# Head sums of a second attention layer in their own step, decay sums by scans on VectorE, and values' transposes later in a unit

## What is computed

```python
# layer 1, gated linear attention: decays of a head's 128 keys, summed along time
log_a = jax.nn.log_sigmoid(p_a @ gla_gate_up[l] + gla_gate_bias[l]) / GLA_TAU
bcum = jnp.cumsum(at, axis=2)                 # differences of these sums decay keys and queries
# layer 2: queries and keys are normed per head of 64 before attention
qa, ka, va, qb, kb, vb = _split(h @ w_in, EVEN_SPLITS)
qa = _rmsnorm(qa.reshape(B, S, A_KV_HEADS, A_GROUP, HEAD_DIM), qn_a)
ka = _rmsnorm(ka.reshape(B, S, A_KV_HEADS, HEAD_DIM), kn_a)
qb = _rmsnorm(qb.reshape(B, S, B_HEADS, HEAD_DIM), qn_b)
kb = _rmsnorm(kb.reshape(B, S, B_HEADS, HEAD_DIM), kn_b)
```

## Time and profile before

| what | value |
|---|---|
| median of 3 runs | 2407.9 us (2406.82 to 2408.54) |
| the profiled execution | 2407.05 us, span 2405.3 us |
| PE busy | 2368.6 us, 98% of the span |
| DVE, ACT, POOL busy | 1315.1, 928.3, 159.4 us (55%, 39%, 7%) |
| PE, layer 2's stretch 1064 to 1210 | busy 130.4 of 146 us |
| weights read | 201.94 MB, 16 DMA engines busy about 28% |

### The profile page before, as it was taken

The page is one execution under the profiler, slowest core; times in us unless marked ns, Lnnn a source line. Parts: engine busy times, 40 slices in busy tenths (PEclk is TensorE's granted clock), DMA queues, the critical chain, the costliest instruction groups (busy, mean ns, idle before and its releaser), DMA issues.

```text
span 2405.3 us, 32851 instructions
## 1 busy us (share of the span) xinstructions
PE 2368.6 (98%) x13012; PEld 1922.5 (80%) x13012; DVE 1315.1 (55%) x1928; ACT 928.3 (39%) x1459; POOL 159.4 (7%) x197
## 2 busy tenths in 40 slices
PE   8999999999999999998999999999999999999999
PEld 6787777787888888875678888888888887888887
DVE  7666555878653443567764334356655556534433
ACT  5444553447242332446554223233322223422321
POOL 5111100000000000052220000000000000100000
PEclk9999999999999999999999999999999999999999
DMA  4222222222323333321023233232222212323322
GB/s 158 71 71 71 67 67 88 78 64 82 103 88 97 105 89 97 102 88 44 25 83 112 88 97 105 87 92 83 80 70 88 79 53 79 113 89 105 96 87 79
DMA packets 60639, 205.80 MB, mean 86 GB/s; under 512 B 7249, under 2 KB 7249, under 8 KB 60386
## 3 DMA queue, kind: packets, MB, share of 16 engines
q1 hardware_dynamic: 59760, 202.93, 27.6%
q10 hardware_dynamic: 754, 1.14, 0.2%
HBM read 201.94 MB, written 2.10 MB: 85 GB/s over the span
## 4 chain that ended last, share of the span: by engine, by line
PE 52%; DVE 2%; ACT 1%; issue 0%; POOL 0%; POOLq 0%; DVEq 0%; ACTq 0%
PE psum L1651 46%; PE psum L1712 1%; PE psum L1808 1%; PE psum L1719 1%; PE psum L1761 1%; ACT arena L769 1%; PE psum L1729 0%; PE psum L1725 0%; DVE arena L1287 0%; DVE cols L1293 0%; PE psum L1678 0%; PE psum L1779 0%; PE psum L1697 0%; PE psum L1734 0%; POOL stage L637 0%
## 5 line engine op out<-in xcount | busy, mean ns | idle before, releaser
L1651 PE MATMUL psum<-hhi,whi 128*128 128x512 f32 x1640 | 650.0, 396 | 11.8 <-DVE wlo L1014 9.2
L1651 PE MATMUL psum<-hlo,whi 128*128 128x512 f32 x1640 | 643.2, 392 | 0.0
L1651 PE MATMUL psum<-hhi,wlo 128*128 128x512 f32 x1640 | 642.0, 391 | 0.0
L1651 PE MATMUL psum<-uhi,whi 128*128 128x512 f32 x1392 | 548.2, 394 | 0.6 <-DVE arena L1094 0.6
L1651 PE MATMUL psum<-ulo,whi 128*128 128x512 f32 x1392 | 545.6, 392 | 0.0
L1651 PE MATMUL psum<-uhi,wlo 128*128 128x512 f32 x1392 | 545.4, 392 | 0.0
L1014 DVE TENSOR_TENSOR wlo<-raw,whi 128x1024 fp32r<-128x1024 f32 (+1 forms) x399 | 465.6, 1167 | 61.7 <-ACT whi L980 31.9
L1651 PEld LDWEIGHTS psum<-hhi,whi 128*128 128x128 f32 x1640 | 308.5, 188 | 78.6 <-issue 12.3
L1651 PEld LDWEIGHTS psum<-hhi,wlo 128*128 128x128 f32 x1640 | 308.5, 188 | 64.9 <-issue 0.4
L1651 PEld LDWEIGHTS psum<-hlo,whi 128*128 128x128 f32 x1640 | 308.8, 188 | 62.5 <-issue 1.2
L980 ACT CAST whi<-raw 128x1024 fp32r<-128x1024 f32 x190 | 199.9, 1052 | 351.7 <-PE psum L1651 351.7
(11 more groups left out here) (231 smaller groups left out, 1754.0 us busy)
## 6 DMA issues: line engine op xcount, KB each, us to landing
raw<-in_packed_dram SPq DMA_DIRECT2D x359, 512.0 KB, 3.6
raw<-in_packed_dram SPq DMA_DIRECT2D x40, 256.0 KB, 2.6
x<-in_xt_dram SPq DMA_DIRECT2D x8, 256.0 KB, 5.3
out_dram<-x SPq DMA_DIRECT2D x8, 256.0 KB, 2.0
arena<-in_near_bias_dram ACTq DMA_DIRECT2D x1, 1024.0 KB, 5.7
vec<-in_vec_dram ACTq DMA_DIRECT2D x1, 44.0 KB, 4.1
arena<-in_gla_gate_up_dram ACTq DMA_DIRECT2D x1, 32.0 KB
arena<-in_gla_gate_bias_dram ACTq DMA_DIRECT2D x1, 2.0 KB
```

What stands on the lines that cost most here:

```text
L1651: mm = pe.matmul(g, w[:, u % 4, k, :], v[:, k, :], start=n == 0, stop=n == 3 * kt - 1)
```

## The change

It does three things.

1. *Second layer's heads.* `put_off` now holds for heads of the dilated attention ("d") alone. For the heads of layer 2, ACT and DVE do `square_head` first in the next step, ahead of `split_hi` and `split_lo`, PE's sum stands in that same unit at product 13, and root and post follow in the step.
2. *Decay sums.* The product with the gate matrix is turned (keys on the partitions, time along the row), so `lg` leaves each head's log decays in `g_z[h]`, and DVE sums them along time by four scans per head (`sums`, L1342 of the changed kernel; listed below as SCALAR_TENSOR_TENSOR of `ones`), one head beside each of units 53 to 56. `tri`, its products and ACT's copies go.
3. *Values' transposes.* Where a unit holds a head's sum and a value's transposes (units 7, 16, 25 and 34 now), `mark` puts them at products 4 and 16 instead of 6 and 10, and the parts behind 16. In steps of the recurrence with a value before them, the first part comes at product 10 instead of 6, and the others behind it.

```diff
@@ plan
-    todo += zip(gla_head(0), [("decays", i) for i in range(5)] + [("gla", 0, -1)])
+    todo += zip(gla_head(0), [("sums", i) for i in range(4)] + [None, ("gla", 0, -1)])
@@ put_off
-            return gate or units[prev][0] == "head"
+            return gate or prev in HEADU and units[prev][5][0] == "d"
@@ ACT
-                l = g_z[t % 2]
+                l = g_z[t]
                 act.wait_ge(lg_pe, t + 1)
-                if t >= 2:
-                    act.wait_ge(lg_done, t - 1)
...
-                        nc.scalar.copy(g_bs[:, h, :], psum[:, 2 + h, :]).then_inc(gl_b, 1)
...
                 for u, prev, parts in steps[name][OPENING if name == "l1" else 0:]:
+                    if prev in HEADU and not put_off(prev, u):
+                        square_head(prev)
                     if u is not None:
                         split_hi(u + 2)
...
-                    head = prev is not None and units[prev][0] == "head"
+                    head = prev in HEADU and pending is not None
@@ DVE
-                if u >= 2 and units[u - 2][0] in GATES + ("head",):
+                if u >= 2 and put_off(u - 2, u - 1):
                     dve.wait_ge(posted, u - 1)
...
-                dve.scalar_tensor_tensor(out=g_lg[:, t, :], in0=psum[:, 2 + t, :], scalar=0.0, in1=g_z[t % 2],
-                                         op0=ALU.min, op1=ALU.subtract).then_inc(lg_done, 1)
+                l = g_z[t]
+                dve.scalar_tensor_tensor(out=l, in0=psum[:, 2 + t, :], scalar=0.0, in1=l,
+                                         op0=ALU.min, op1=ALU.subtract).then_inc(lg_min, 1)
+
+            def sums(h):
+                dve.wait_ge(lg_min, h + 1)
+                for c in range(NT):
+                    s = slice(P * c, P * c + P)
+                    ins = dve.tensor_tensor_scan(g_bs[:, h, s], ones[:, :], g_z[h][:, s], 0.0, ALU.mult, ALU.add)
+                ins.then_inc(lg_done, 1)
...
-                    dve.wait_ge(gl_b, 4)
+                    dve.wait_ge(lg_done, 4)
...
-                    head = prev is not None and units[prev][0] == "head"
+                    head = prev in HEADU and pending is not None
+                    if prev in HEADU and not head:
+                        square_head(prev)
@@ PE
-                pe.matmul(psum[:, 2 + t, :], g_pa[0:17, P * t:P * t + P], g_up[0:17, :], start=True, stop=True).then_inc(lg_pe, 1)
+                pe.matmul(psum[:, 2 + t, :], g_up[0:17, P * t:P * t + P], g_pa[0:17, :], start=True, stop=True).then_inc(lg_pe, 1)
...
-                pe.wait_ge(lg_done, NT)
-                for c in range(NT):
-                    mm = pe.matmul(psum[:, 2 + h, P * c:P * c + P], g_lg[:, c, P * h:P * h + P], tri[:, :], start=True, stop=True)
-                mm.then_inc(gl_b_pe, 1)
...
+            def mark(i, n, total, lead, turned):
                 if i == 0:
                     return 0
+                if turned and i < 3:
+                    return (total // 6, 2 * total // 3)[i - 1]
+                if turned:
+                    return 2 * total // 3 + total * (i - 2) // (3 * (n - 2))
...
-                    if prev in TURNS:
+                    if prev in TURNS or prev in HEADU and not put_off(prev, u):
+                        lead = lead if shared else 13 if prev in HEADU else 10
                         shared.append(("shared_bank", prev))
-                    head = prev if prev in HEADU else None
+                    head = prev if prev in HEADU and put_off(prev, u) else None
                     lead = lead if shared else 0
+                    both = len(shared) == 2
```

More of the change, by code:

```diff
@@ L318, in build @@
         g_head = [gla_head_places()]
-        g_lg = place(NT, 4 * P)
+        g_bs = place(4, SEQ)
         g_head.append(gla_head_places())
@@ L326, in build @@
         g_sq = [v for h in range(4) for v in g_head[h % 2][0:2]]
-        g_bs = g_lg.rearrange("p c (h k) -> p (c h k)", h=4).rearrange("p (h t) -> p h t", h=4)
         g_a = place(NT, P)
@@ L337, in build @@
         g_pa, g_up = g_kt.rearrange("p a b -> p (a b)"), g_a.rearrange("p a b -> p (a b)")
-        tri = sb("tri", [P, P])
         g_mask = sb("g_mask", [P, 6, 32])
@@ L342, in build @@
         up_in, pa_ones, lg_pe, lg_ln, lg_done = sem("up_in"), sem("pa_ones"), sem("lg_pe"), sem("lg_ln"), sem("lg_done")
-        gl_b_pe, gl_b, gl_d, gl_e, gl_f = sem("gl_b_pe"), sem("gl_b"), sem("gl_d"), sem("gl_e"), sem("gl_f")
+        lg_min, gl_d, gl_e, gl_f = sem("lg_min"), sem("gl_d"), sem("gl_e"), sem("gl_f")
         gl_level, gl_a, gl_kt_pe, gl_kt = sem("gl_level"), sem("gl_a"), sem("gl_kt_pe"), sem("gl_kt")
@@ L546, in _ @@
                                     pattern=[[-1, P]], channel_multiplier=1))
-            done(pool.memset(tri[:, :], 1.0))
-            done(pool.affine_select(out=tri[:, :], in_=tri[:, :], compare_op=ALU.is_ge, fill=0.0, base=0,
-                                    pattern=[[1, P]], channel_multiplier=-1))
             done(pool.memset(d_pick, 0.0))
@@ L867, in nothing @@
                 pass
-            PARTS = {"ret": ret, "rates": rates, "att": att, "bias": bias, "lg": lg, "gla": gla, "decays": decays, "mask": nothing}
+            PARTS = {"ret": ret, "rates": rates, "att": att, "bias": bias, "lg": lg, "gla": gla, "sums": nothing, "mask": nothing}
             def static(name):
@@ L1472, in bias @@
                 dve.wait_ge(dve_step, chain.up())
-            PARTS = {"ret": ret, "rates": rates, "att": att, "bias": bias, "lg": lg, "gla": gla, "mask": mask,
-                     "decays": lambda i: None}
+            PARTS = {"ret": ret, "rates": rates, "att": att, "bias": bias, "lg": lg, "gla": gla, "mask": mask, "sums": sums}
             def static(name):
@@ L1910, in gla @@
                     pe.matmul(MB, ones[:, :], g_sq[2 * h], start=True, stop=True).then_inc(gl_sum, 1)
-            def decays(h):
-                if h == 4:
-                    return
-                pe.wait_ge(lg_done, NT)
-                for c in range(NT):
-                    mm = pe.matmul(psum[:, 2 + h, P * c:P * c + P], g_lg[:, c, P * h:P * h + P], tri[:, :], start=True, stop=True)
-                mm.then_inc(gl_b_pe, 1)
             def nothing(*_):
                 pass
-            PARTS = {"ret": ret, "rates": nothing, "att": att, "bias": nothing, "lg": lg, "gla": gla, "decays": decays, "mask": mask,
+            PARTS = {"ret": ret, "rates": nothing, "att": att, "bias": nothing, "lg": lg, "gla": gla, "sums": nothing, "mask": mask,
                      "shared_bank": shared_bank}
-            def mark(i, n, total, lead):
+            def mark(i, n, total, lead, turned):
                 if i == 0:
                     return 0
+                if turned and i < 3:
+                    return (total // 6, 2 * total // 3)[i - 1]
+                if turned:
+                    return 2 * total // 3 + total * (i - 2) // (3 * (n - 2))
                 if lead and n > 2:
@@ L1963, in static @@
                         if u is not None:
-                            products(u, mark(i, n, total, lead), mark(i + 1, n, total, lead), *operand)
+                            products(u, mark(i, n, total, lead, both), mark(i + 1, n, total, lead, both), *operand)
                         PARTS[part[0]](*part[1:])
                     if u is not None:
-                        products(u, mark(n - 1, n, total, lead), total, *operand)
+                        products(u, mark(n - 1, n, total, lead, both), total, *operand)
                     if u == steps[name][0][0]:
```

## The result

| | before | changed |
|---|---|---|
| median of 5 runs | 2407.9 us (2406.75 to 2408.54) | 2394.52 us (2393.72 to 2395.09) |
| profiled execution | 2407.05 us, span 2405.3 | 2394.59 us, span 2392.9 |

The ratio is 0.9946 (95% interval 0.9932 to 0.9960): faster by 0.5%. Measured a second time (experiment 12), the changed kernel took 2394.69 us beside 2408.34 of before.

What follows compares the result with a forecast made beforehand. PE, busy 98% of the span, was taken as the bound, so only fewer PE instructions or waits help. Decay sums 3.6, transposes 1.6 and second-layer heads 6.9 make 12.1 us: 2407.05 - 12.1 = 2395.0, range 2387 to 2404.

Steps and rivals of the forecast that it cites:

- Part 1: Units 53 to 56: DVE scans, hidden beside the units, replace sixteen `tri` products; 0.90 us each, 3.6 us saved.
- Part 2: Units 16, 25 and 34: values' transposes move to product 16, their waits for ACT go; net 1.6 us saved.
- Part 3: Second layer's heads squared and summed in their own step: 6.9 us saved; bounds 19 us gained to 5.2 lost.
- old waits: Second layer, four head sums: PE's waits for ACT's square go, with draining 10.5 us saved.
- start: Second layer's first softmax no longer stands behind the last head's post and two copies: PE's waits shrink by 4.0 us.
- crowding: Second layer's attention parts come four products apart instead of eight: eight more waits of 0.5 us, 4.0 us lost.
- clock: Unit 177: the granted clock no longer falls if PE doesn't stand so long; 1.6 us saved.
- new waits: Second layer's head sums: PE waits for late squares, 3.0 us in unit 172, 1.4 in unit 173; together 5.4 lost.
- Transposes: Second layer's values: waits for ACT go, 2.9 us saved; at product 10 they wait for their unit's evacuation, 2.7 lost.
- slower rival: Units 171 to 181: ACT's square is late at all eight heads, kernel slower, 2414 us; 4 in 100.
- clock rival: Clock falls after unit 172's wait; two such falls cost 3.2 us more, 2398.2 us; 10 in 100.
- item chain: Second layer's attention chain on DVE and ACT bounds; PE's waits only move, heads' change gives nothing: 2401.8 us; 15 in 100.

Runs made afterwards that it cites:

- experiment 12: The changed kernel measured once more, unaltered, for the scatter between executions on the same chip: 2394.69 us, ratio 0.9943 to the kernel before.
- experiment 3: Changed kernel without the later values' transposes, marks of before in units 7, 16, 25, 34 and beside the recurrence: 2394.28 us.
- experiment 4: Changed kernel with the value's transposes at product 13 instead of 16 and the attention parts behind them back at 15 and 19: 2393.40 us.
- the heads alone: Kernel before with only the second layer's heads moved into their own step, decay sums and values' transposes unchanged: 2396.94 us, ratio 0.9955.
- experiment 5: Changed kernel with the second layer's head sums at product 6 of their unit instead of 13: 2409.24 us, ratio 1.0004 to the kernel before.
- experiment 9: Changed kernel with layer 1's transposes and parts at 4, 13, 15 and 19, and sums in units 166 and 172 at product 20: 2393.18 us.
- experiment 7: Changed kernel with head 171's sum at product 20 of unit 172 instead of 13, its parts at 21 and 22: 2393.68 us.
- experiment 8: Changed kernel with the second layer's transposes at product 14 instead of 10, parts behind them at 17 and 20: 2393.69 us.
- experiment 10: Changed kernel with one attention part beside unit 171 and three beside 172, instead of two and two: 2395.28 us.
- experiment 2: Kernel before with part 3 of the diff and nothing of parts 1 and 2: 2396.94 us, ratio 0.9955.

## Why the prediction was right, and where it was not

2395.0 was forecast and 2394.52 measured, with the likeliest case's mechanism. Part 1 was right; the errors of parts 2 and 3 cancel in good part, so that the total came within 0.5 us is in part luck.

- **Part 1**, 3.6 us: 3.7 in the profile, 3.4 by its own run. The scan was taken as 0.42 us from the 128x256 row and measures 0.40; the cover was there, and even twice the scans fit under a unit. The fourfold price can be ruled out. The Trainium skill (DVE: opcode table, instruction layouts, handler registers and perf-mode slots, section Datapath and trigger behaviour) says that the built-in scan runs at half throughput; the trace agrees, since a scan of 128 elements takes 0.40 us, about what a 128x256 operation takes (0.42).
- **Part 2**, 1.6 us: 0. The step "they move from product 10 to product 16, so these waits go" was right (0.45 to 0.51 each). What failed is what I didn't cost: the parts behind the transposes move with them, their softmax reaches DVE and POOL later, and PE pays 0.52 in the next unit, in unit 17 0.28 of it waiting for POOL and 0.24 for DVE's evacuation. Experiments 3 and 4 show it from both sides. The move of the recurrence's parts cost nothing, as said (units 66 to 76 shorter by 0.05).
- **Part 3**, 6.9 us: 9.25 in the profile, 11.1 in its own run. The *old waits* at the sums are gone altogether, and so are the transposes' waits for ACT. In both profiled executions the time of units 165 to 190 can be divided without a rest, by what stands between one product and the next (each time runs from the start of the product before to the start of the product behind):

| between two products, units 165 to 190 | before, us | changed, us | difference | forecast |
|---|---|---|---|---|
| 13 sums of heads | 19.74 | 13.88 | -5.86 | -10.5 + 5.4 |
| 5 times a value's transposes | 6.95 | 5.64 | -1.31 | -2.9 + 2.7 |
| attention parts in units 171 and 172 (*start*) | 10.21 | 7.41 | -2.80 | -4.0 |
| attention parts in units 173 to 190 (*crowding*) | 65.07 | 66.44 | +1.37 | +4.0 |
| nothing, or the norm's sum (*clock*) | 114.07 | 113.42 | -0.65 | -1.6 |

  - *Sums*: one takes 0.68 without a wait. The four old waits cost 10.5, as forecast, and a fifth place, in unit 183, 0.4. Of new waits unit 172 lost 2.8 (3.0 forecast), unit 173 0.8 (1.4, which allowed 0.5 for draining where the others had 0.75), unit 181 0.7 (0.5) and unit 166 0.7 (0.5), together 5.0 of 5.4.
  - *Transposes*: 0.59 without a wait. The new waits cost 1.14, 0.91 and 0.65 at the three places named, 2.7 as forecast. The old ones cost 4.0 and not 2.9, since the transposes in unit 177, for which no wait was named, lost 0.84 at the lower clock.
  - *Start*: the named waits of 1.23, 2.13 and 0.70 became one of 0.48, 3.6 less, but the parts are only 2.8 shorter, since the clock now falls among them. With the heads alone, at full clock but with a wait of 1.93 for POOL, it is 2.3.
  - *Clock*: what the fall in unit 177 had cost went, but a new fall came in unit 172, so little of the 1.6 is left.
  - *Crowding* was the mis-sized term: 1.4 and not 4.0. Instead of eight more waits of 0.5 us there are two at L1758 (0.32 and 0.53), and those at L1805 are 1.7 where L1808 had 1.5. Why so few came isn't shown.
  - *Together*: the sums (0.8), the transposes (1.1) and the crowding (2.6) were set 4.5 us too low as a gain, the start (1.2) and the clock (0.95) 2.15 too high. That leaves the 2.35 by which part 3 was short.
- **The slower rival** has the right mechanism and is kept away by the mark: with the sum at 6 instead of 13 (experiment 5), where PE waits before the sum of every head, 14.7 us are lost and the change is worth nothing. Less wait per head than I put is enough, because the second product waits for DVE too and heads 165 to 169 pay as well.
- **The clock rival** was half true: one fall in either profiled execution of the change, none in the heads alone. Of the 1.7 us that the fall takes by the windows only 0.6 reaches units 172 and 173 (28.7 us against 28.1). The Trainium skill (TensorE: Matmul & The Clock Gate, section What's actually happening) says that the array's clock is halved once PE has idled; the trace agrees in part: here it fell after a wait of 1.99 us (the change) and one of 2.39 (experiment 9), and not after one of 2.40 (experiment 7).
- **The item chain** bounds what is left: three edits that took away the named wait of unit 172 or those before the transposes (experiments 7, 8, 10) found it again at POOL or DVE. It didn't bound the kernel before in the way that the rival had it: part 3 alone, with DVE's and ACT's work the same, gave 11.1 us (experiment 2).

## What to carry to other kernels

A mark that is moved carries everything that stands behind it: follow the last of these to its reader in the next unit before the gain is counted. When a wait in a chain over several engines goes, ask which one is next and how much later it is; here most of a named wait of 2.0 us came back at another engine, and 0.3 was won in the units concerned. Work that stands behind an engine's long step is late for everyone: an earlier place in ACT's and DVE's queues, with PE's sum one unit earlier, was worth some 10 us, a later mark on PE alone nothing.

## What was not expected of the hardware

The first unit took between 6.89 and 8.36 us in the fourteen profiled executions, though its code is the same in all of them. It begins with products 0.43 us apart, six of them in the shortest and thirteen in the longest, then 0.23; this is the end of the slow stretch in the changed kernel, with thirteen:

```profile
13.25 0.63 PE L1648 MATMUL psum<-hhi,wlo 128*128 128x512 f32 x1
13.68 0.63 PE L1648 MATMUL psum<-hhi,whi 128*128 128x512 f32 x1
14.11 0.47 PE L1648 MATMUL psum<-hlo,whi 128*128 128x512 f32 x1
14.42 0.39 PE L1648 MATMUL psum<-hhi,wlo 128*128 128x512 f32 x1
```

That is 1.5 us of scatter at the start of a kernel alone, a third of what I had called measurable and as much as part 2 was thought to bring. With the clock's falls in the second layer (none, one or two in an execution), it is why differences under 1 us were read here from units and not from medians.
